# A recurrence with dense 64x64 chunk matrices, and its group norm woven into the output projection

## The reference

```python
# per head: S_t = S diag(w_t) + (S a_t) b_t^T + v_t k_t^T ;  y_t = S_t r_t
y = rwkv7_scan(rh, heads(decay), kh, vh, -kk, kk * a)
mu = jnp.mean(y32, axis=-1, keepdims=True)              # over the 64 of a head
var = jnp.mean(jnp.square(y32 - mu), axis=-1, keepdims=True)
y = ((y32 - mu) * lax.rsqrt(var + LNX_EPS)).reshape(B, T, H * D) * ln_w + ln_b
o_rwkv = (y + bonus) * g
mix = jnp.concatenate([o_fox, o_rwkv], axis=-1) @ w_out
h = h + rmsnorm(mix, attn_norm_post)
```

## Time and profile before

| | |
|---|---|
| time, median of 3 runs | 3662.53 us (3649.61 to 3670.58) |
| the profiled execution | 3656.49 us, its span 3654.7 us |
| stage A | 367.5 to 522.2 us of the span |
| stage B | 522.2 to 556.8 |
| stage C | 556.8 to 589.9 |
| stage D, to the start of block 2 | 589.9 to 624.5 |

### The profile page before, as it was taken

How to read it: one execution, slowest core, us unless ns; L and a number is a source line. 1 busy time by engine, 2 the same in 40 slices (tenths; PEclk the granted TensorE clock), 3 DMA queues, 4 the chain that set the end, 5 groups by cost and what they waited for, 6 DMA issues and landing times.

```text
span 3654.7 us, 47335 instructions
## 1 busy us (share of the span) xinstructions
PE 3479.7 (95%) x16942; PEld 2829.5 (77%) x16942; DVE 1820.7 (50%) x3463; ACT 1243.3 (34%) x1637; POOL 802.9 (22%) x334
## 2 busy tenths in 40 slices
PE   8998998799988989998999999999999899999998
PEld 6665996588766778887887888788888688888886
DVE  3564442433115552333113499998888254444443
ACT  2223211333235543334224333354544233323332
POOL 6430001244432323333444344400000000000000
PEclk9988999899999999999999999999999999999999
DMA  3110000122221112222223244455555655555542
GB/s 128 56 37 0 1 2 22 54 98 98 88 97 63 57 63 75 75 75 69 91 94 100 81 145 146 130 180 173 181 172 185 224 198 190 198 203 201 196 143 75
DMA packets 145931, 407.80 MB, mean 112 GB/s; under 512 B 11176, under 2 KB 43944, under 8 KB 143536
## 3 DMA queue, kind: packets, MB, share of 16 engines
q1 hardware_dynamic: 73472, 265.85, 22.7%
q10 hardware_dynamic: 72368, 140.68, 10.7%
HBM read 337.28 MB, written 69.21 MB: 111 GB/s over the span
## 4 chain that ended last, share of the span: by engine, by line
PE 83%; DVE 13%; ACT 2%; issue 1%; ACTq 1%; DMA 1%; DVEq 0%
PE bank L325 22%; PE bank L327 22%; PE bank L326 22%; PE bank L857 2%; PE bank L855 1%; PE bank L354 1%; DVE arena L1664 1%; PE bank L556 1%; ACT arena L898 1%; PE bank L791 1%; PE bank L542 1%; PE bank L465 1%; DVE arena L1793 1%; PE bank L427 1%; PE bank L546 1%
## 5 line engine op out<-in xcount | busy, mean ns | idle before, releaser
L325 PE MATMUL bank<-xs,ring_hi 128*128 128x512 f32 x2488 | 996.8, 401 | 63.7 <-DVE xs L1372 31.1
L327 PE MATMUL bank<-xs,ring_lo 128*128 128x512 f32 x2488 | 975.6, 392 | 0.0
L326 PE MATMUL bank<-xs,ring_hi 128*128 128x512 f32 x2488 | 975.0, 392 | 0.0
L1343 POOL TENSOR_TENSOR ring_lo<-ring,ring_hi 128x1024 fp32r<-128x1024 f32 x262 | 650.7, 2486 | 1062.6 <-ACT ring_hi L898 1062.6
L898 ACT ACTIVATE arena<-bank 128x512 f32<-128x512 f32 (+5 forms) x612 | 408.3, 698 | 1143.6 <-PE bank L327 745.1
L898 ACT ACTIVATE ring_hi<-ring 128x1024 fp32r<-128x1024 f32 x469 | 495.5, 1059 | 504.4 <-DMA ring<-weights 241.3
L325 PEld LDWEIGHTS bank<-xs,ring_hi 128*128 128x128 f32 x2488 | 471.1, 189 | 174.1 <-issue 38.2
L327 PEld LDWEIGHTS bank<-xs,ring_lo 128*128 128x128 f32 x2488 | 470.7, 189 | 101.9
L326 PEld LDWEIGHTS bank<-xs,ring_hi 128*128 128x128 f32 x2488 | 471.9, 190 | 98.6 <-issue 4.6
L1806 DVE TENSOR_TENSOR ring_lo<-ring,ring_hi 128x1024 fp32r<-128x1024 f32 x206 | 252.3, 1225 | 404.4 <-ACT ring_hi L898 404.4
L325 PE MATMUL bank<-gw,ring_hi 128*128 128x512 f32 x1024 | 398.5, 389 | 0.7 <-ACT arena L898 0.7
(11 more groups left out here) (271 smaller groups left out, 4049.1 us busy)
## 6 DMA issues: line engine op xcount, KB each, us to landing
ring<-weights SPq DMA_DIRECT2D x503, 512.0 KB, 3.3
hidden<-arena ACTq DMA_DIRECT2D x128, 256.0 KB, 3.9
gates<-arena ACTq DMA_DIRECT2D x16, 2048.0 KB, 6.6
arena<-hidden ACTq DMA_DIRECT2D x16, 2048.0 KB, 10.7
arena<-gates ACTq DMA_DIRECT2D x16, 2048.0 KB, 17.2
xres<-x_t ACTq DMA_DIRECT2D x4, 512.0 KB, 5.8
out_t<-arena SPq DMA_DIRECT2D x1, 2048.0 KB, 7.1
arena<-ret_decay ACTq DMA_DIRECT2D x1, 1024.0 KB, 5.6
```

The lines of the kernel that those rows point to most:

```text
L325: pe.matmul(out_, wh, x[0], start=start, stop=False, skip_group_check=True)
L326: pe.matmul(out_, wh, x[1], start=False, stop=False, skip_group_check=True)
L327: return pe.matmul(out_, wl, x[0], start=False, stop=stop, skip_group_check=True)
L1343: pool.tensor_tensor(ring_lo[:, r, :], ring[:, r, :], ring_hi[:, r, :].bitcast(F32), ALU.subtract).then_inc(lo_done, 1)
```

## The change

Each 128x128 matrix with two 64x64 blocks on its diagonal is stored as those two blocks alone: block `p` on partitions 64p to 64p+63, and the columns of its partition half hold 4 groups of head 0 and then 4 of head 1. One tile of 512 columns so holds a pair of heads, where it held one head. `quad` picks a block, `chunks` makes the 16 products 64x64x64 of one such tile.

- Stage A: the loop now runs over two rounds `r`, each with two pairs `s` in alternation. A level has 32 + 16 small products per pair (16 + 16 on the last), and two `keep_clock(7, 1)`. The copies and additions keep their size, but each serves two heads. Masks are one addition of an identity and strided products with 64-column masks, which six small DVE copies build inside the constants near the start of the kernel.
- Stage B: the scores are 16 small products per chunk for both matrices, with one mask. The old state is added by PE (products with the identity, `state`), the product of keys and values is issued a chunk ahead (`keys`), and only `removal` waits for `UU`. DVE scales straight from PSUM; banks 7 and 4 alternate.
- Stage C: all products are 64x64x64, two pairs at a time, in two halves per round; four banks in place of two; the second half waits with `st.sync` for the first to be complete.
- Stage D: the mean product of a pair waits for that pair's `YY` alone; the splits of the other mixer's output stand earlier on ACT; gain, bias and gate are folded into `BON` and `RG` beforehand; the variance sums stand inside `w_out_block(0)`, after its first half; the spreads stand before `w_out_block(1)`, and each pair's spread and each pair's two DVE operations are released by themselves, with its part's split right behind.

```diff
...
-        HS = [[40, 41, 42, 43, 44, 45, 46, 47], [48, 49, 70, 71, 72, 73, 74, 50]]
+        HS = [[42, 41, 40, 43, 44, 45, 46, 47], [70, 49, 48, 71, 72, 73, 74, 50]]
...
-        RW_PE, RW_ACT, RW_DVE = 28, 16, 12
+        RW_PE, RW_ACT, RW_DVE = 28, 18, 12
...
+
+            def quad(ap, p, j, g):
...
+            def chunks(dst, l, r):
+                for j in range(2):
+                    for c in range(NCH):
+                        g, p = c // 2, c % 2
+                        mm = pe.matmul(quad(dst, p, j, g), quad(l, p, j, g), quad(r, p, j, g), start=True, stop=True,
+                                       skip_group_check=True)
+                return mm
...
+            for r in range(2):
+                for s in range(2):
+                    m, b0 = 2 * r + s, 3 * s
...
+                    for c in range(NCH):
+                        g, p = c // 2, c % 2
+                        cols = slice(c * C, (c + 1) * C)
+                        for k, (l, r_) in enumerate(((TB, TA), (TA, TB))):
+                            for e in range(2):
+                                rows = slice(e * HD, (e + 1) * HD)
+                                pe.matmul(quad(bank[b0 + e], p, k, g), tile(l + m)[rows, cols], tile(r_ + m)[rows, cols],
+                                          start=True, stop=True, skip_group_check=True)
+                    for c in range(NCH):
+                        g, p = c // 2, c % 2
+                        cols = slice(c * C, (c + 1) * C)
+                        for e in range(2):
+                            rows = slice(e * HD, (e + 1) * HD)
+                            mm = pe.matmul(quad(bank[(b0 + 2, 7 - s)[e]], p, e, g), tile(TK + m)[rows, cols],
+                                           tile(TA + m)[rows, cols], start=True, stop=True, skip_group_check=True)
+                    mm.then_inc(rw_pe, 1)
+                for lev in range(5):
+                    for s in range(2):
+                        hs, b0 = HS[s], 3 * s
+                        a, b = (0, 1) if lev % 2 == 0 else (1, 0)
+                        pe.wait_ge(rw_dve, 8 + RW_DVE * r + 2 * lev + s + 1)
+                        if s == 0:
+                            keep_clock(7, 1)
+                        mm = chunks(bank[b0], tile(hs[2 + a]), tile(hs[a]))
+                        if lev < 4:
+                            mm = chunks(bank[b0 + 1], tile(hs[a]), tile(hs[2 + a]))
+                        mm.then_inc(rw_pe, 1)
+                    for s in range(2):
+                        hs, b0 = HS[s], 3 * s
+                        a, b = (0, 1) if lev % 2 == 0 else (1, 0)
+                        if s == 0:
+                            keep_clock(7, 1)
+                        pe.wait_ge(rw_act, 36 + RW_ACT * r + 2 * lev + s + 1)
+                        chunks(bank[b0 + 2], tile(hs[b]), tile(hs[4 + a])).then_inc(rw_pe, 1)
...
+            def state_part(c, part):
+
+                g, p = c // 2, c % 2
+                trow = slice(p * HD, (p + 1) * HD)
+                for h in range(8):
+                    m, e = h // 2, h % 2
+                    rows = slice(e * HD, (e + 1) * HD)
+                    if part == "keys":
+                        l, r_ = v4(tile(MK + m))[trow, g, rows], v4(tile(MV + m))[trow, g, rows]
+                    elif part == "state":
+                        l, r_ = cc("ident")[rows, rows], shv[rows, c, m * HD:(m + 1) * HD]
+                    else:
+                        l, r_ = v4(tile(MB + m))[trow, g, rows], tile(UU + g)[trow, h * HD:(h + 1) * HD]
+                    mm = pe.matmul(bank[SBANK[c % 2]][rows, m * HD:(m + 1) * HD], l, r_,
+                                   start=(part == "keys" and h < 2), stop=(part == "removal"), skip_group_check=True)
+                return mm
...
+            state_part(0, "keys")
             for c in range(NCH):
...
+                keep_clock(3, 1)
+                trow = slice(c % 2 * HD, (c % 2 + 1) * HD)
                 if c > 0:
...
+                    pe.wait_ge(rw_dve, base_dve + 3 * c)
                     for h in range(8):
                         m, e = h // 2, h % 2
                         rows = slice(e * HD, (e + 1) * HD)
                         mm = pe.matmul(bank[6 - e][trow, m * HD:(m + 1) * HD], tile(WT + m)[rows, c * C:(c + 1) * C],
                                        shv[rows, c, m * HD:(m + 1) * HD], start=True, stop=True, skip_group_check=True)
                     mm.then_inc(rw_pe, 1)
-                head_scores(c, 0)
+                    if c < NCH - 1:
+                        st.go(state_part(c, "state"))
+                head_scores(c)
+                if c + 1 < NCH - 1:
+                    state_part(c + 1, "keys")
                 if c < NCH - 1:
-                    pe.wait_ge(rw_dve, base_dve + 4 * c + 1)
...
-                head_scores(c, 1)
-            bp, bd, ba = base_pe + 30, base_dve + 31, base_act
-
-            keep_clock(4, 2)
+                    pe.wait_ge(rw_dve, base_dve + 3 * c + 1)
+                    st.sync()
+                    state_part(c, "removal").then_inc(rw_pe, 1)
...
+                h, rows, trow = 2 * m + e, slice(e * HD, (e + 1) * HD), slice(p * HD, (p + 1) * HD)
+                v = v4(tile(MV + m))[trow, g, rows] if part == 0 else tile(UU + g)[trow, h * HD:(h + 1) * HD]
+                pe.matmul(bank[4 + m][rows, (2 * g + p) * C:(2 * g + p + 1) * C], v, quad(tile(MS[h]), p, part, g),
+                          start=start, stop=True, skip_group_check=True)
+
+            def y_state(m, e, c):
+
+                rows, cols = slice(e * HD, (e + 1) * HD), slice(c * C, (c + 1) * C)
+                return pe.matmul(bank[4 + m][rows, cols], shv[rows, c, m * HD:(m + 1) * HD], tile(TR + m)[rows, cols],
+                                 start=False, stop=True, skip_group_check=True)
+
+            for r in range(2):
+                for half in range(2):
+                    keep_clock(3, 2)
+                    if half:
+                        st.sync()
+                    for g in range(TT):
+                        for part in range(2):
+                            for e in range(2):
+                                for s in range(2):
+                                    y_local(2 * r + s, (half + s) % 2, g, e, part, half == 0 and g == 0 and part == 0)
+                    for c in range(1, NCH):
+                        for s in range(2):
+                            mm = y_state(2 * r + s, (half + s) % 2, c)
+                    if half == 0:
+                        st.go(mm)
                 mm.then_inc(rw_pe, 1)
...
             for m in range(NPAIR):
-                pe.wait_ge(rw_act, ba + 4)
+                pe.wait_ge(rw_act, ba + m + 1)
                 pe.matmul(bank[4 + m][:, :], cc("bmean"), tile(YY + m), start=True, stop=True).then_inc(rw_pe, 1)
...
+            def variance_sums():
+
+                for m in range(NPAIR):
+                    pe.wait_ge(rw_act, ba + m + 1)
+                    head_sums(4, m, tile(GNS + m)).then_inc(rw_pe, 1)
...
+                    if b == 0 and a == 0:
+                        variance_sums()
...
             w_out_block(0)
             for m in range(NPAIR):
-                pe.wait_ge(rw_act, ba + m + 1)
-                head_sums(4, m, tile(GNS + m)).then_inc(rw_pe, 1)
+                pe.wait_ge(rw_inv, 2 + m)
+                spread(GNR, m, 4 + m).then_inc(rw_inv_out, 1)
             w_out_block(1)
-            pe.wait_ge(rw_inv, 2)
-            for m in range(NPAIR):
-                mm = spread(GNR, m, 4 + m)
...
             for k in range(4):
                 A(XS[k][0], tile(OF + k), ACT.Copy).then_inc(hi_ready, 1)
+            bp = 36 + RW_PE * 2 + 22
+            ba = 36 + RW_ACT * 2
+            for m in range(NPAIR):
+                act.wait_ge(rw_pe, bp + m // 2 + 1)
+                A(tile(YY + m), bank[4 + m][:, :], ACT.Copy).then_inc(rw_act, 1)
...
+            for a, b in (("strict", "incl_T"), ("strict_T", "ident")):
+                st(CP(cc(a)[HD:P, 0:C], cc(a)[HD:P, C:P]))
+                st.go(CP(cc(a)[0:HD, C:P], cc(b)[0:HD, 0:C]))
+                st.go(CP(cc(a)[HD:P, C:P], cc(b)[HD:P, C:P]))
...
+                        ve.wait_ge(rw_act, 36 + RW_ACT - 1 + s)
+                    for e in range(2):
+                        half = slice(e * 256, (e + 1) * 256)
+                        st.go(TTN(arena[:, hs[2]:hs[0] + 1:hs[0] - hs[2], half].rearrange("p k (g t) -> p k g t", t=C),
+                                  bank[b0 + e][:, :].rearrange("p (k g t) -> p k g t", k=2, t=C), both, ALU.mult))
+                    for e in range(2):
+                        half = slice(e * 256, (e + 1) * 256)
+                        st.go(TTN(tile(hs[6])[:, half].rearrange("p (g t) -> p g t", t=C),
+                                  bank[(b0 + 2, 7 - s)[e]][:, half].rearrange("p (g t) -> p g t", t=C),
+                                  mask8("strict_T", 0)[:, 0:TT, :], ALU.mult))
```

(56 more changed lines are left out.)

187 lines of the change are left out of this document (62 added, 125 removed).

## The result

| | time, median | ratio to before, 95% interval |
|---|---|---|
| before | 3657.5 us (4 runs) | |
| changed | 3549.2 us (3540.7 to 3556.4, 4 runs) | 0.9694 [0.9666, 0.9722] |

A forecast was written before the change was run, and what follows sets the result against it. PE, busy for 95% of the span, was taken as the bound; terms of -65.3, -5.0, -18.5, -11.9 and +1.0 sum to -99.7 us, giving 3556.8 or 3562.8, called 3559 us, range 3532 to 3605.

The forecast's parts named there:

- The price of a small record: PE's 64-column records: 31 ns where array parts alternate, 55 where they don't; 31 taken for all 3616.
- My lower bound: Lower end of the forecast's own range, 3535 us: 27 ns a record, no contention, prelude 0.
- Stage A: Two rounds of 44.7 us, 89.4 against 154.7, with levels of 6.8 us: -65.3 us.
- Nothing waits: Inside a level of stage A, ACT's copies and the additions are done before PE wants them; level 6.8 us.
- Stage B: A chunk takes 3.8 us, was 4.3; stage 29.6 us, was 34.6: -5.0 us.
- Stage C: 368 small records at 31 ns plus `keep_clock` and `st.sync`, 14.6 us, was 33.1: -18.5 us.
- Stage D: Block 2 counts as started at 24.2 us after PE's end of y, was 34.6; -11.9 with its slow start spared.
- The stall: In stage D, block 2 waits 2.4 us for its last part, DVE's operations being lengthened 2.9 us beside POOL.
- Rival 1: Records alternating rows within one bank (`chunks`, `MV`, B's `state`) run at 55 ns: +51 us, 3610; chance 0.11.
- Rival 2: Long series, everywhere, bound by issue, not the array: at 65 ns a record +23, 3680 us; chance 0.05.
- Rival 3: Clock falls to its lower level in A and B: 3677 us, or about 3600 if partial; chance 0.06.
- Rival 4: Something between, fetch stalls or waits now and then in the long series, 40 ns a record: +33, 3592; chance 0.11.

The follow-up runs named there:

- Experiment 1: Changed kernel with six series of its own 64x64x64 products, on one, two or four array parts, put before stage B; one execution, 3572.7 us.
- experiment 2: Changed kernel with `chunks` issuing all 8 products of one partition half, then all 8 of the other; 3611.9 us, ratio 0.9855 to the kernel before.
- 4: Changed kernel without any `keep_clock` in stages A, B and C; 3541.1 us, ratio 0.9687 to the kernel before.

## Why the prediction was right, and where it was off

The mechanism held: PE's records set stages A, B and C, and what they lost in time went through to the end. Of the 115.8 us, 114.8 are found in the four stages and ahead of them. The forecast of 3559 us was 10 us over the median; the sum, taken between the two traces, fell short by 15.1.

**The price of a small record** is the step that was mis-sized. I bounded it by 31 and 55 ns, took 31 for every record and wrote that parts "alternate". That is right, or nearly, for the 2048 records of `chunks` and the `MV` product and for those of stage B and of C's state products. But 768 records (opening 384, closing `WT` product 128, C's local products 256) go round four parts. Experiment 1 gives 16 ns for these, 768 x 15 = 11.5 us less work for PE. Not all of it shortens the kernel: the opening of each round's second pair, 192 of the records, runs while DVE masks the first pair, which leaves 576 x 15 = 8.6 us of the 15.1 (4.8 in A, 3.8 in C); the rest is mostly stage B's. My lower bound had 27 ns for all, which happens to cover it.

**Stage A**: the level of 6.8 us was 6.75, the last level 4.8 as predicted. The opening took 4.6 us to the first level's start, not 6.1, mostly by the four-part price, and the closing 4.7, not 6.0, of which that price explains 1.0; a round was 41.5, not 44.7. The wait for the second pair's masks, for which I had 0.6 us, came inside the first level, which took 7.0 and 7.2 us. "Nothing waits" holds for the other levels. DVE's masks kept the opening from being shorter still.

**Stage B**: a chunk took 3.2 us, not 3.8. PE's 96 records took 2.7 us, where I had 3.0 and 0.25 for the last one's end. The trace shows records of one group among those of the next (`L646` and `L628` from 455.63 to 455.86 us), so I take it that a group that begins on other parts overlaps the tail of the one before; no run tests this. The way from PE over DVE back to PE was 0.53, as predicted (0.52), and the score mask just filled the time until `removal` was done.

**Stage C**: 10.3, not 14.6; 256 local records at 17 instead of 31 ns are 3.6 of the 4.3 us.

**Stage D**: 24.0 against 24.2 us. The stall is there and at its size: the last part came 2.6 us late (2.4 predicted), and POOL's split lengthened two operations by 3.2 us in all (2.9 predicted):

```profile
505.26 1.90 POOL L1377 TENSOR_TENSOR ring_hi<-ring,cst 128x1024 fp32r<-128x1024 f32 x1 [265.43 <-DMA ring<-weights]
...
506.04 1.67 DVE L1663 TENSOR_TENSOR arena<-arena 128x512 f32<-128x512 f32 x1
...
507.24 2.72 POOL L1381 TENSOR_TENSOR ring_lo<-ring,ring_hi 128x1024 fp32r<-128x1024 f32 x1
...
507.64 2.87 DVE L1417 TENSOR_TENSOR xs<-arena,xs 128x512 fp32r<-128x512 f32 x1
```

**Rival 1** (one bank) fell: the diagonal in one bank and in two banks both run at 31 ns. The rule of the Trainium skill's TensorEngine Tiling page (section Restrictions and Gotchas) does not slow this case, where the two sets of rows write to different partitions of the bank; two sets of rows on the same partitions of one bank were not tried. **Rival 2** (issue) fell: 256 records ran in a row at 16 ns. The Trainium skill's page TensorE: Matmul & The Clock Gate (section "Wait — 56ns, not 53.3ns?") names 62 ns for decoding in software, which this series excludes here. **Rival 3** (the clock) did not come about here, but in experiment 2 it did, and for a short stretch in 4. **Rival 4** is not needed.

Open: why the clock stayed low for one round of experiment 2 and not for the other (by their times, three of its four executions had a low round); and what the single edits in stage D are worth beside the order of PE's work, some 6 us together.

## What to carry to other kernels

Count the parts of the array that successive small products use: from record to record it costs 60 ns over 1, 2 or 4 parts (64 columns, float32), so block-diagonal work in an order that stays on one part would lose what it saves (the estimate of 154 us for stage A), and four parts are twice as good as two. The order may keep two parts for 8 records (15 ns in the opening), but 16 on one part already cost 50 ns each. Look in the trace for rows of each such case before one price is taken for all. A call that keeps the clock up costs its own time and the change of kind (9.5 us for twenty here): try without it where different parts work side by side all the time; where PE waits it may pay, as the low clock at the start of C shows.

## What was not expected of the hardware

- The price does not depend on which two parts alternate, nor on the bank: 31 ns in four different pairings.
- PE can be busy 100% of the time and stay at the lower clock for 83 us (372 to 455 us in experiment 2, 64x64 records mostly on one part), and run the same instructions at the upper level in the next round.
- The length of a DVE operation beside POOL turned on which of the two started first: the same cast took 0.42 us when it started 0.12 us ahead of POOL's operation and 2.05 us when it started 0.13 us behind it (two executions, not tested further). So 5.1 us of copies taken out of that stretch gave `L404` about 3 us in two executions and nothing in a third.
